# A gated hybrid encoder layer: softmax reciprocals spread by two DMAs instead of by matmuls

## The reference

```
h    = rmsnorm(x) ; proj = h @ w_in
A:   probs = softmax([scores * scale + alibi, sink])       # within |t - s| <= 128
     o_a   = (probs @ v_a) * silu(z_a)
C:   o_c   = (softmax(q_c @ k_mem / 16) @ v_mem) * silu(z_c)
B:   o_b   = gelu(u) * (w_s @ layernorm(gelu(v)) + b_s) * silu(z_b)
x    = x + ((o_a @ w_br_a) * g_a + (o_b @ w_br_b) * g_b + (o_c @ w_br_c) * g_c) @ w_out
out  = rmsnorm(x) * final_gain
```

## Time and profile before

| | us |
|---|---|
| median of 3 runs | 2721.03 (2720.34 to 3223.52) |
| the profiled execution: its time | 2720.84 |
| the profiled execution: span of its slowest core | 2719.1 |
| TensorE busy | 2681.4, 99% of the span |
| VectorE, ScalarE, GpSimd busy | 826.2, 606.2, 204.4 |
| TensorE's granted clock, mean of every core | 0.999 of 2.4 GHz |

### The profile page before, as it was taken

The page is one execution under the profiler, slowest core; times in us unless marked ns, Lnnn a source line. Parts: engine busy times, 40 slices in busy tenths (PEclk is TensorE's granted clock), DMA queues, the critical chain, the costliest instruction groups (busy, mean ns, idle before and its releaser), DMA issues.

```text
span 2719.1 us, 35622 instructions; the slowest of 8 cores (2714.6 to 2719.1 us)
## 1 busy us (share of the span) xinstructions
PE 2681.4 (99%) x13427; PEld 1258.4 (46%) x13427; DVE 826.2 (30%) x1381; ACT 606.2 (22%) x1197; POOL 204.4 (8%) x389
## 2 busy tenths in 40 slices
PE   8999999999999999999999999999999999999998
PEld 4444455444444444444444444544444444444444
DVE  6230066423622222222450002754163111122225
ACT  3221244333111111110121113443411111111012
POOL 1000101001000000000000000000000000000000
PEclk9999999999999999999999999999999999999999
DMA  9844656325455554445995444231544444444475
GB/s 213 167 76 75 109 97 113 67 48 94 70 109 109 108 101 78 71 77 100 262 241 98 75 77 70 48 55 33 95 75 73 75 74 76 76 78 78 78 201 155
DMA packets 77591, 270.29 MB, mean 99 GB/s; under 512 B 8688, under 2 KB 9072, under 8 KB 76144
## 3 DMA queue, kind: packets, MB, share of 16 engines
q0 software_dynamic: 55440, 201.74, 43.7%
q1 hardware_dynamic: 21984, 66.27, 7.5%
HBM read 452.92 MB, written 16.78 MB: 173 GB/s over the span
## 4 chain that ended last, share of the span: by engine, by line
PE 95%; DMA 2%; ACT 1%; DVE 1%; issue 1%; POOL 0%; SPq 0%; DVEq 0%; ACTq 0%; POOLq 0%
PE ps L337 91%; DMA RG<-wall 1%; PE ps L820 1%; PE ps L944 1%; DMA OT<-xs 1%; PE ps L891 1%; PE ps L860 1%; PE ps L1014 0%; PE ps L987 0%; PE ps L1120 0%; DVE ps L824 0%; ACT AR L827 0%; DVE GN L874 0%; ACT AR L994 0%; ACT AR L1057 0%
## 5 line engine op out<-in xcount | busy, mean ns | idle before, releaser
L337 PE MATMUL ps<-hT,RG 128*128 128x512 bf16 (+1 forms) x7296 | 1629.4, 379 | 1.9 <-ACT KEEPV L372 0.9
L337 PEld LDWEIGHTS ps<-hT,RG 128*128 128x128 bf16 x7296 | 708.5, 98 | 826.3 <-issue 4.2
L337 PE MATMUL ps<-OT,RG 128*128 128x512 bf16 x2048 | 458.4, 380 | 0.0
L287 POOL DMA_DIRECT2D RG<-wall x384 | 203.6, 531 | 2450.6 <-PE ps L337 2068.6
L1159 ACT ACTIVATE GN<-ps 128x512 f32<-128x512 f32 x192 | 114.1, 596 | 897.3 <-PE ps L337 896.9
L337 PEld LDWEIGHTS ps<-OT,RG 128*128 128x128 bf16 x2048 | 200.0, 98 | 241.0
L1167 DVE TENSOR_TENSOR GN<-ps,GN 128x512 f32<-128x512 f32 x128 | 88.5, 692 | 551.0 <-PE ps L337 515.4
L337 PE MATMUL ps<-RG,AR 128*128 128x512 bf16 (+1 forms) x1072 | 228.5, 376 | 0.0
L337 PE MATMUL ps<-RG,hT 128*128 128x512 bf16 x1008 | 221.2, 380 | 3.2 <-DMA RG<-wall 3.2
L824 DVE TENSOR_TENSOR ps<-ps,ND 128x384 f32<-128x384 f32 (+1 forms) x192 | 101.7, 551 | 328.2 <-PE ps L820 327.4
L337 PEld LDWEIGHTS ps<-RG,AR 128*128 128x128 bf16 x1072 | 104.8, 98 | 123.2
(11 more groups left out here) (127 smaller groups left out, 1076.2 us busy)
## 6 DMA issues: line engine op xcount, KB each, us to landing
RG<-wall POOLq DMA_DIRECT2D x384, 512.0 KB, 6.4
OT<-xr SPq DMA_DIRECT2D x16, 1024.0 KB, 17.5
y<-OT SPq DMA_DIRECT2D x30, 512.0 KB, 5.7
OT<-xs SPq DMA_DIRECT2D x8, 1024.0 KB, 11.4
HX<-xr SPq DMA_DIRECT2D x16, 512.0 KB, 6.2
OT<-xt SPq DMA_DIRECT2D x16, 512.0 KB, 19.3
OT<-xh SPq DMA_DIRECT2D x4, 512.0 KB, 14.7
OT<-mt SPq DMA_DIRECT2D x4, 512.0 KB, 28.7
```

Source lines behind the costliest of these rows:

```text
L287: S.op("pool", lambda h: h.dma_start(out=RG[:, sl, :], in_=wall[row * 128:(row + 1) * 128, :]), r=list(gate), w=["R%d" % sl], dma=True)
L337: ins = h.matmul(psb(b, n), lhsT=pairs[i][0], rhs=pairs[i][1], start=(i == 0), stop=(i == N - 1))
```

## The change

The reciprocal no longer goes through TensorE. `total` now leaves its sums in a buffer `RV` of its own (two halves, `k` 0 and 1, in turn). `invert` takes the reciprocal and issues two transfers on SP's queue: 4 rows of 256 values to a scratch row `inv` in HBM, and that row of 1024 values back into `rb`, 128 partitions wide (512 KB). For an A head, GpSimd multiplies `rb` by the gate in place (`scale`, two instructions of 128x512), and `gate` is a single VectorE operation that is run one slot later (`fin`). For a C head there is no GpSimd work and no later slot; `gate2` keeps two VectorE operations. `spread`, `split`, ScalarE's copy for it, `SEL` and `low` are gone. `rb` is one of two 4 KB parts of `GN` for an A head, and always the first part for a C head. `side` places `total` behind three score pieces instead of one, and the last two C heads get 24 and 20 matmuls of `v0` between their sums and their first value step instead of 12.

```diff
             def invert(self):
-                r, hi = self.r, self.hi
+                r = self.r
                 S.op("dve", lambda hh: hh.reciprocal(out=r, in_=r), w=self.rc)
-                S.op("act", lambda hh: hh.activation(out=hi, in_=r, func=AF.Copy), r=self.rc, w=self.hic)
...
-            def spread(self, s):
...
-            def gate(self, s, dst, dstc, b):
...
+                k = self.k
+                spdma(inv_d[k, :].rearrange("(q n) -> q n", n=256), r[0:128:32, :], r=self.rc, w=["inv%d" % k])
+                spdma(self.rb, inv_d[k:k + 1, :].broadcast_to([128, 1024]), r=["inv%d" % k], w=self.rbc)
+
+            def scale(self, s, src, srcc):
+
+                t = self.rb[:, s * 512:(s + 1) * 512]
+                S.op("pool", lambda hh: hh.tensor_tensor(out=t, in0=t, in1=src, op=ALU.mult), r=srcc,
+                     w=self.rbc[4 * s:4 * s + 4])
+
+            def gate(self, s, dst, dstc):
+
+                b, t = self.b[s], self.rb[:, s * 512:(s + 1) * 512]
                 S.op("dve", lambda hh: hh.tensor_tensor(out=dst, in0=psb(b, 512), in1=t, op=ALU.mult),
-                     r=self.tc, w=dstc + pc(b))
+                     r=self.rbc[4 * s:4 * s + 4], w=dstc + pc(b))
+
+            def gate2(self, s, dst, dstc, b, i):
+
+                t, tc = view("GN", 4096 + i * 2048, 512, F32), cel("GN", 4096 + i * 2048, 2048)
+                S.op("dve", lambda hh: hh.tensor_tensor(out=t, in0=self.rb[:, s * 512:(s + 1) * 512], in1=dst,
+                                                        op=ALU.mult), r=self.rbc[4 * s:4 * s + 4] + dstc, w=tc)
+                S.op("dve", lambda hh: hh.tensor_tensor(out=dst, in0=psb(b, 512), in1=t, op=ALU.mult),
+                     r=tc, w=dstc + pc(b))
...
-            return [sm.total, sm.invert, sm.split], [half(0)], [half(1)]
+            return [sm.total, inv], [half(0), half(1)], [fin(0), fin(1)]
...
-                    return (sc[:1] + pv[0][:1] + sc[1:2] + pv[0][1:2] + sc[2:3] + pv[0][2:] + sc[3:5] + pv[1] + sc[5:7] +
-                            pv[2] + sc[7:])
+                if len(sc) == 8:
+                    return (sc[:3] + pv[0][:1] + sc[3:4] + pv[0][1:] + sc[4:5] + fin[:1] + sc[5:6] + fin[1:] +
+                            pv[1][:1] + sc[6:] + pv[1][1:])
+                return fin + pv[0][:1] + sc[:1] + pv[0][1:] + sc[1:] + pv[1]
...
             weave(v0[4:8], p14[0])
-            weave(v0[8:12], p14[1] + p15[0])
-            weave(v0[12:16], p14[2])
-            run(p15[1])
-            run(v0[16:18])
-            run(p15[2])
-            run(v0[18:])
+            run(v0[8:10])
+            weave(v0[10:16], p14[1])
+            run(p15[0])
+            run(v0[16:20])
+            weave(v0[20:24], p15[1])
+            run(v0[24:])
```

More of the change, by code:

```diff
@@ L883, in spread @@
-            def spread(self, s):
-                b = bank("pv")
-                self.b[s] = b
-                def emit(hh):
-                    ins = None
-                    for k in range(2):
-                        q = 2 * s + k
-                        ins = hh.matmul(psb(b, 256, k * 256), lhsT=SEL[:, q * 128:(q + 1) * 128], rhs=self.rl,
-                                        start=(k == 0), stop=True, skip_group_check=True)
-                    return ins
-                S.op("pe", emit, r=["sel"] + self.rlc, w=pc(b))
@@ L947, in f, with fin, inv @@
                     S.op("pe", emit, r=sorted(set(cells)), w=pc(b))
-                    sm.spread(s)
-                    oa, oac = ot_slab(h, s)
-                    sm.gate(s, oa, oac, b)
-                return f
-            return [sm.total, sm.invert, sm.split], [half(0)], [half(1)]
+                    sm.b[s] = b
+                return f
+            def fin(s):
+                return lambda: sm.gate(s, *ot_slab(h, s))
+            def inv():
+                sm.invert()
+                for s in range(2):
+                    sm.scale(s, *ot_slab(h, s))
+            return [sm.total, inv], [half(0), half(1)], [fin(0), fin(1)]
         def c_off(c):
@@ L1018, in f @@
                     S.op("pe", emit, r=VC_ALL + ecl, w=pc(b))
[L1019 to L1020 removed]
                     oc, occ = ot_slab(24 + c * 2 + dc, s)
[L1022 removed]
+                    sm.gate2(s, oc, occ, b, dc)
                 return f
[L1024 removed]
+            return [sm.total, sm.invert], [step(0, 0), step(0, 1), step(1, 0), step(1, 1)], []
         def kv_mem(i):
@@ L1380, in side @@
                 sc, pv = [], []
+                fin = late.pop() if late else []
                 if 0 <= i - 1 < 16:
@@ L1456, in _consts @@
     ident = np.eye(128, dtype=np.float32)
-    sel = np.zeros((128, 4, 128), np.float32)
-    for i in range(4):
-        sel[32 * i:32 * i + 2, i, :] = 1.0
-    low = np.where(np.arange(128) % 2 == 1, -1.0, 0.0).astype(np.float32).reshape(128, 1)
     bf = ml_dtypes.bfloat16
-    return nd.astype(bf), ident, sel.reshape(128, 512).astype(bf), low
+    return nd.astype(bf), ident
 def _stationary(m, c0):
```

43 lines of the change are left out of this document (11 added, 32 removed).

## The result

The changed kernel takes **2715.7 us** (median of 15 runs), the kernel before 2720.6 beside it on the same chip: a ratio of 0.9981, with a 95% interval of 0.9973 to 0.9989. It is faster by about 5 us, where 20 were forecast: inside the range, and a quarter of the gain. (Medians are over all runs; ratios and means, and the time of the last experiment, leave out runs in which one die was held at a lower clock.)

A forecast was written before the change was run, and what follows sets the result against it. TensorE bounds the kernel, busy 2681.4 of 2719.1 us. From 2720.84, 28.7 for spreads and waits of the sums goes off, 2 for gates and 6.6 for tails come on: 2701 us, range 2690 to 2730.

The forecast's parts named there:

- What leaves TensorE: TensorE in the attention: spreads worth 13.8 us and waits of the sums worth 14.9 go, together 28.7 us.
- Product, transfers alone: A head's new path: store taken as 2.5 us, broadcast 4.5, GpSimd product 1.4; nothing waits.
- Cover: ... 0 to 3 us once, I take 0: GpSimd's queue: weight loads held behind products are covered by the 8-chunk ring; little room only in memory-value slots.
- two further signs: In the changed profile, a product over 3 us or a broadcast over 8 us makes the prediction wrong.
- My upper ends (3.1 and 6.2): Longest times assumed for the 4 KB store (3.1 us) and the 512 KB broadcast (6.2 us).
- rival 4: Slow round trip: 20 us for the broadcast among queued transfers, about 2910 us; chance 0.05, over 2775.
- Tail: Last two C heads of each tile: waits of 6.3 us in place of 3, +3.3 a tile, +6.6 in all.
- A head's slack of 2 us: A heads' gates have little room before their bank is wanted: 0.1 us on 22 heads, between 0 and 5.
- rival 2: Half late: broadcast 6.2 and product 2.5 make the second tile's second product 1.6 late; 2710 to 2720 us, chance 0.12.
- Rival 5: The sums still wait, for a bank or an exp, at the new place; 15 us stay, 2716 us; chance 0.04.
- rival 1: Everything is hidden: short transfers, no gate late, tail at its lower end; 2696 us, chance 0.12, at or below 2695.
- rival 3: The wait replaces the spread, all four prices at upper ends: 2751 us, slower; chance 0.11, 2721 to 2760.

The follow-up runs named there:

- both edits: The changed kernel with GpSimd's products recorded behind the slot's weight loads and the sums of the last two C heads placed early: 2693.7 us, ratio 0.9899.
- the new order alone: The kernel before with only the sums moved behind three score pieces and the last score piece ahead of the second value half, spreads kept: 2712.9 us, ratio 0.9969.
- the filled waits: The changed kernel with 6, 4 and 10 unused matmuls ahead of the three waiting instructions of each tail: 2713.7 us, ratio 0.9967.
- the memory's values apart: The kernel with late product and early tail sums, plus the memory values' second half moved from A head 10's slot to 11's: 2693.7 us, ratio 0.9896.
- the row three times: The kernel with late product and early tail sums, each head's broadcast issued three times, each behind the landing before: 2910.2 us, ratio 1.0649.
- the first four experiments: Product behind weight loads (2708.8 us), tail's sums early (2700.7), both together (2693.7), and the sums moved in the kernel before (2712.9).

## Why the prediction was wrong, and what of it held

**What leaves TensorE: right.** Spreads and waits of the sums are gone, the slot is 10.07 us for 10.0, the second tile's A and C stage 172.5 to 175.7 for 174.3. Nothing waits for an exp. The 28.7 us are borne out by the fastest cores with both edits, 33 under for 34.5, and by the mean of cores 0 to 3 without the value loads, 34.3 under. They hold together only: the new order alone, priced at 14.9, brought 8, because the spreads then wait.

**Product, transfers alone: right.** 1.147 us for 1.4; the estimate of 1.1 from the Trainium skill, "GPSIMD Engine Reference", section 3 (its 4497 ns are for an addition), agrees with the trace. The page has such work some two times slower than on VectorE, here it is 1.7 times (1.147 for 0.692). That length fitted: with the product behind the loads no slot of the second tile is late. What it cost was its place in a queue. The store alone takes 1.7 us for 2.5, under my lower end, the broadcast 3.5 to 4.4 to its product for 4.5.

**The step that failed is "Cover: ... 0 to 3 us once, I take 0".** I had seen that loads stand behind the product and that five chunks in a slot leave a few us. I priced that as the delay of one load. I did not ask what the held loads do once they go: they meet the next head's store and broadcast, on the same DMA engines. The store then takes 4 to 7 us and the broadcast 9 to 12, far from the 2.5 and 4.5 that I took as if each were alone, so the next product is late, and the next burst too. That is 14 us on core 4, in four slots of the first tile, and 8.3 us on the mean core. The prediction's own sign of a wrong cover, a wait for a weight load in the memory slots, is there with 2.33 and 2.11 us. The edit that takes the product from ahead of the loads gave 8 us back, and leaving out the value loads took 8 from the longest stage. On the mean core the two parts of the step come apart: that stage takes 205.1 us, 201.6 with the product behind the loads, and 196.4 where nothing waits. So some 4 us are held loads, and some 5 are round trips that meet loads which nothing held. Of two further signs, a broadcast over 8 us came true and a product over 3 us did not. My upper ends (3.1 and 6.2) were under what the queue does to them; the earlier trace rows, up to 28.0 for a queued landing, was the row to use for the slots with five loads, and I kept it for rival 4.

**Tail: the waits right on core 4, the sum too small.** 5.9 us of waits listed and 3 x 0.16 exposed make 6.4 for 6.3. Each tail of core 4 is 1 to 3 us over the forecast; on the mean core, where the first tail's waits are shorter, it is 0.2 and 0.8. The missing term is the half clock, 1.7 us a stretch, one in most tails and two in core 4's first; the filled waits show it apart from the waits.

**A head's slack of 2 us: too large.** Where the round trip is not disturbed, the slot has no wait. The 2 us hide some of the loss elsewhere.

**The metric is the slowest of eight.** I forecast one core. Taken from the mean core before, 2716.6, my gain of 20.1 gives 2696.5; the mean core came out at 2705.5, 9.0 over. The slowest core stands 8.1 us above the mean, where it stood 2.5 above it before: 5.6 more. So of the 14.6 us over the forecast span some 8 are lateness in the first tile's A and C stage, 1 is in the tails, and 5.6 are that the lateness falls unevenly, on another core each time. This last part has no term in my sum.

**Rivals.** The time, 2715.7, is that of rival 2 (half late, 2710 to 2720), and its mechanism, a second product behind its due time, is what happened, but in the first tile, where it gave no loss, and by transfers beside loads, not by a product of 2.5 us. Rival 5 is excluded by the waits, rivals 1, 3 and 4 by the time.

**Open:** why single cores are still late in the first tile with both edits and no value loads, by 4 us (core 2) and 7 (core 5). Long broadcasts stand ahead of core 5's long slots, but what makes them long on one core in one run was not isolated. The burst of five is not needed for it: on core 4 of the changed kernel the broadcast issued at 408.91 took 10.5 us to its product with two loads just ahead of it. Loads of other cores, which run at the same time, are a rival that no run here tests.

## What to carry to other kernels

Before a compute instruction is put on a queue that also issues loads, ask what the held loads will collide with when they are released together. Price a small transfer on the path by what is queued when it is issued (here 1.7 us alone, up to 7.3 beside loads), not by its bytes. Record the waiting instruction behind the loads that don't need it. And price an idle gap of TensorE with the clock that follows it, and the slowest core rather than a typical one.

## What the hardware showed that was not expected

- On core 4 of the changed kernel a 4 KB store to HBM took 1.7 us in quiet stretches and mostly 3.6 to 7.3 with 512 KB weight loads issued shortly before it. A broadcast of 512 KB took some 4 us to its product in quiet stretches, 9.1 and 11.8 in the two slots with a burst of five loads, and once 10.5 beside two.
- After the pair of waits of 1.53 and 0.87 us, whose ends are 1.46 us apart, the granted clock was 0.50 for 3.4 us. A wait of 1.73 us alone in the kernel before, and one of 1.75 on core 5 of the changed kernel, had no such stretch behind them; a wait of 3.50 and one of 3.57 had. The length alone does not decide it: on core 1 waits of 3.17 (ended at 489.95) and 3.07 us (578.79) had none, on core 3 one of 2.51 (1870.40) had.
- In the experiment without the store the granted clock was 0.81 in stretches of up to 15.2 us outside the attention. The values there are not the layer's, but they are not needed for it: the filled waits, the memory's values apart and the row three times, whose values are right, have such stretches too, at the same moments on cores 4 and 5 and on cores 6 and 7, and the profiles of the changed kernel, the kernel before and the first four experiments have none. What sets them off was not tested.
